# An encoder layer for two request groups: the sample's tiles first through attention and routing, its selection beside the prompt's out-projection

## What is computed

```python
h = rms_norm(x) ; p = h @ w_in
a = BiGLA(p[gla columns])            # 4 heads, chunked gated linear attention, both directions
d = DiffAttn(p[diff columns])        # 4 heads, softmax(q1 k1) - lam * softmax(q2 k2), rotary, QK-norm
x = x + concat(a, d) @ w_out
h2 = rms_norm(x)
aff = softmax(h2 @ w_router)         # 16 experts
gates, idx = top_k(aff.T, cap)       # per expert: 32 rows of the prompt, 64 of the sample
y[idx] += gates * (silu(h2[idx] @ w_gate) * (h2[idx] @ w_up)) @ w_down      # summed over 16 experts
```

## Time and profile before

| | us |
|---|---|
| median of 3 runs | 1534.68 (1534.57 to 1535.32) |
| the profiled execution | 1534.62 |
| its span | 1532.8 |
| PE busy | 1501.5 (98%) |
| DVE busy | 1245.4 (81%) |
| ACT busy | 1090.7 (71%) |
| POOL busy | 140.4 (9%) |
| mean of DMA traffic | 292 GB/s |

### The profile page before, as it was taken

One profiled execution on the slowest core, in us unless ns is written; L12 is line 12 of the kernel. 1 busy time (PEld: TensorE's weight loads), 2 busy tenths in 40 slices (PEclk: granted clock), 3 DMA queues, 4 the chain that ended last, 5 costly groups with the idle time before them and its releaser, 6 DMA issues.

```text
span 1532.8 us, 18601 instructions
## 1 busy us (share of the span) xinstructions
PE 1501.5 (98%) x7293; PEld 1228.2 (80%) x7293; DVE 1245.4 (81%) x1133; ACT 1090.7 (71%) x1230; POOL 140.4 (9%) x105
## 2 busy tenths in 40 slices
PE   7999999999999999999999999999999999999997
PEld 7787777678878888888888888888888888888886
DVE  4358679775588898888989888888988888898985
ACT  7555456875357878787787778778777878778784
POOL 1013131000000101010110101011010101101010
PEclk9999999999999999999999999999999999999999
DMA  6111101402759999999999999999999999999992
GB/s 233 56 55 56 56 1 56 154 28 81 269 200 389 376 388 372 396 374 393 380 384 384 378 395 377 393 380 385 383 378 394 380 393 375 390 383 385 393 375 74
DMA packets 191990, 447.98 MB, mean 292 GB/s; under 512 B 13016, under 2 KB 13344, under 8 KB 191904
## 3 DMA queue, kind: packets, MB, share of 16 engines
q1 hardware_dynamic: 187488, 433.03, 75.8%
q0 software_dynamic: 3968, 12.65, 3.6%
q10 hardware_dynamic: 448, 1.12, 0.2%
HBM read 434.19 MB, written 12.58 MB: 291 GB/s over the span
## 4 chain that ended last, share of the span: by engine, by line
PE 92%; DVE 4%; ACT 1%; issue 1%; DMA 0%; POOLq 0%; POOL 0%; DVEq 0%; ACTq 0%
PE ps L952 23%; PE ps L954 23%; PE ps L953 23%; PE ps L619 5%; PE ps L621 5%; PE ps L620 5%; PE ps L987 1%; PE ps L841 1%; PE ps L875 1%; DVE states L1502 1%; PE ps L945 1%; PE ps L861 1%; PE ps L897 1%; DVE slice_low L1410 1%; PE ps L927 0%
## 5 line engine op out<-in xcount | busy, mean ns | idle before, releaser
L1840 DVE TENSOR_TENSOR wl<-raw,wh 128x2048 fp32r<-128x2048 f32 x384 | 873.0, 2289 | 126.1 <-ACT wh L1345 124.6
L1345 ACT CAST wh<-raw 128x2048 fp32r<-128x2048 f32 x384 | 731.2, 1913 | 125.6 <-PE ps L954 123.5
L952 PE MATMUL ps<-wh,XTh 128*128 128x512 f32 x1024 | 404.9, 395 | 0.9 <-issue 0.9
L954 PE MATMUL ps<-wl,XTh 128*128 128x512 f32 x1024 | 399.5, 390 | 0.0
L953 PE MATMUL ps<-wh,XTl 128*128 128x512 f32 x1024 | 398.5, 389 | 0.0
L954 PEld LDWEIGHTS ps<-wl,XTh 128*128 128x128 f32 x1024 | 192.2, 188 | 41.1
L952 PEld LDWEIGHTS ps<-wh,XTh 128*128 128x128 f32 x1024 | 192.3, 188 | 38.8 <-issue 1.1
L953 PEld LDWEIGHTS ps<-wh,XTl 128*128 128x128 f32 x1024 | 192.5, 188 | 38.1
L952 PE MATMUL ps<-wh,gTh 128*128 128x512 f32 x512 | 200.9, 392 | 0.0
L954 PE MATMUL ps<-wl,gTh 128*128 128x512 f32 x512 | 199.5, 390 | 0.0
L953 PE MATMUL ps<-wh,gTl 128*128 128x512 f32 x512 | 199.2, 389 | 0.0
(11 more groups left out here) (244 smaller groups left out, 1573.0 us busy)
## 6 DMA issues: line engine op xcount, KB each, us to landing
raw<-in_w_gate SPq DMA_DIRECT2D x128, 1024.0 KB, 9.5
raw<-in_w_up SPq DMA_DIRECT2D x128, 1024.0 KB, 9.4
raw<-in_w_down SPq DMA_DIRECT2D x128, 1024.0 KB, 9.6
slice_raw<-in_w_in SPq DMA_DIRECT2D x5, 2048.0 KB, 8.0
X<-in_x_sample SPq DMA_DIRECT2D x8, 512.0 KB, 11.2
slice_raw<-in_w_out SPq DMA_DIRECT2D x2, 2048.0 KB, 8.8
X<-in_x_prompt SPq DMA_DIRECT2D x4, 512.0 KB, 4.4
slice_raw<-in_w_in SPq DMA_DIRECT2D x4, 512.0 KB, 7.8
```

What stands on the lines that cost most here:

```text
L952: pe.matmul(out, hi, rhs_h, start=first, stop=False)
L954: return pe.matmul(out, hi, rhs_l, start=False, stop=last)
L1345: act.copy(wh[:, n % CONV, :], raw[:, n % RAW, :]).then_inc(s_wh, 1)
L1840: dve.tensor_tensor(wl[:, n % CONV, :], raw[:, n % RAW, :], wh[:, n % CONV, :].bitcast(F32), ALU.subtract).then_inc(s_wl, 1)
```

## The change

The order of tiles becomes 2, 3, 4, 5, 0, 1 in the last projection slice, in the attention steps and in all that follows, and the tables are written anew for it. The sample's tiles have their out-projection (`dhalf`) inside the attention loop, and of the fills the prompt's first `turn` falls on iteration 22, its second on 26.

The prompt's four `half` pieces leave the loop. They stand behind it (`gla_half`), and the `dhalf` of the same tile adds on top of it in the same PSUM bank, so that one addition on DVE serves both. They alternate with the sample's `rows_turned` and logits. The softmax and the selection are made in two parts: the sample's eight rounds (64 partitions) stand on DVE between the additions, the root and the norm of the prompt's tiles; the prompt's four rounds (32 partitions) come last. The first round reads PSUM, without the copy that stood ahead of it. POOL lists the values that ACT listed. The rows are stored in two DRAM tensors, and each expert has two gathers, 64 rows and 32. `keep_busy` has 34 matmuls instead of 64. In the projections a third tile's turn comes one iteration later.

```diff
+ORDER = (2, 3, 4, 5, 0, 1)
-        21: ("half", 4, 1), 22: ("half", 5, 0), 23: ("half", 5, 1)}
-FILL[21].append(("dturn", 0, 0))
-FILL[23].append(("dturn", 1, 0))
-FILL.update({24: [("dhalf", 0, 0)], 25: [("dhalf", 0, 1)], 26: [("dhalf", 1, 0)], 27: [("dhalf", 1, 1)]})
...
+        18: [("dhalf", 2, 1)], 19: [("dturn", 4, 0), ("dhalf", 3, 0)], 20: [("dhalf", 3, 1)], 21: [("dhalf", 4, 0)],
+        22: [("dhalf", 4, 1), ("turn", 0, 0)], 23: [("dturn", 5, 0)], 24: [("dhalf", 5, 0)], 25: [("dhalf", 5, 1)],
+        26: [("turn", 1, 0)]}
...
-        return {3: (v0,), 4: (v0 + 1, v0 + 2)}.get(t, ())
+        return {3: (v0,), 4: (v0 + 1,), 5: (v0 + 2,)}.get(t, ())
...
-        ATT = [(g, h, t) for g in range(2) for t in range(GROUPS[g][1]) for h in range(HEADS)]
+        ATT = [(g, h, t) for g in (1, 0) for t in range(GROUPS[g][1]) for h in range(HEADS)]
...
+            pe.wait_ge(s_wtc, len(ATT))
+            gla_half(0, 0, LAST_BANK[0, 0], None)
+            rows_turned(3)
+            pe.wait_ge(*fill_read(last_in_bank(7)))
+            router_logits(2)
+            rows_turned(4)
+            router_logits(3)
+            rows_turned(5)
+            router_logits(4)
+            pe.wait_ge(s_pvc, len(ATT))
+            gla_half(0, 1, LAST_BANK[0, 1], None)
+            router_logits(5)
+            diff_turned(0)
+            pe.wait_ge(*fill_read(last_in_bank(6)))
+            gla_half(1, 0, LAST_BANK[1, 0], None)
             pe.wait_ge(s_aff, 1)
...
+            gla_half(1, 1, LAST_BANK[1, 1], None)
+            pe.wait_ge(s_mtd, POS[0] + 1)
+            diff_turned(1)
+            diff_half(0, 0, None)
+            diff_half(0, 1, None)
+            diff_half(1, 0, None)
+            rows_turned(0)
+            router_logits(0)
+            diff_half(1, 1, None)
+            rows_turned(1)
+            router_logits(1)
...
-            keep_busy(38)
...
-            keep_busy(26)
+            keep_busy(34)
...
+            affinity_exp(afft[:, :, 0:2, 0:NE], 1)
+            diff_high(1)
+            rows_squared(0)
+            h2_copied(0, 0)
+            h2_copied(0, 1)
+            rows_inverse_root(0)
+            rows_squared(1)
+            h2_copied(1, 0)
+            rows_inverse_root(1)
+            affinity_exp(afft[:, :, 2, 0:NE], 2)
...
+            for c in range(0, CAP_S, 8):
+                top_eight(both, c, ps[both, 7, 2 * P:4 * P] if c == 0 else aff[both, :], c // 8 + 1, c + 8 < CAP_S)
+                if c == 8:
+                    diff_low(1)
+                elif c == 16:
+                    diff_half_added(0, 0)
+                elif c == 24:
+                    diff_half_added(0, 1)
+                elif c == 32:
+                    root_refined(0)
                     rows_normed(0)
+                elif c == 40:
+                    diff_half_added(1, 0)
+                elif c == 48:
+                    diff_half_added(1, 1)
+            h2_copied(1)
...
+            for c in range(0, CAP_P, 8):
+                top_eight(rest, c, ps[rest, 2, 0:2 * P] if c == 0 else aff[rest, :], CAP_S // 8 + c // 8 + 1, c + 8 < CAP_P)
+            dve.transpose(pidx[0:CAP_P, :], topi[rest, 0:CAP_P]).then_inc(s_route, 1)
+            dve.transpose(gate[rest, :], topv[rest, 0:CAP_P]).then_inc(s_tables, 1)
```

More of the change, by code:

```diff
@@ L131, in link, with build @@
         self.own()
[L134 removed]
+def build(nc, a, y_prompt, y_sample, h2_prompt, h2_sample):
     ctx = ExitStack()
@@ L354, in build @@
                 b = 6 + u - (len(UNITS) - 2)
-            elif kind == "rope" and t % NT < 3:
+            elif kind == "rope" and t % NT < 2:
                 b = 6 + t % 2
             else:
-                b = sum(x[0] != "rope" or x[2] % NT >= 3 for x in UNITS[:u]) % 4
+                b = sum(x[0] != "rope" or x[2] % NT >= 2 for x in UNITS[:u]) % 4
             EARLIER.append(max((w for w in range(u) if BANKS[w] == b), default=None))
@@ L863, in _ @@
                     mm.then_inc(s_wt, 1)
+                if i == len(ATT) + 3:
+                    rows_turned(2)
                 if i >= len(ATT):
-                    for x in FILL[i]:
+                    for x in FILL.get(i, ()):
                         fill(x)
@@ L923, in _ @@
+            pe.wait_ge(s_aff, 2)
+            for j in range(2):
+                mm = pe.transpose(ps[0:GR, 2, j * P:(j + 1) * P], afft[:, j].rearrange("p g e -> p (g e)"), ident[:])
             mm.then_inc(s_afT, 1)
@@ new lines, in h2_copied, with affinity_exp @@
+            def h2_copied(v, f):
+                p = POS[v]
+                act.wait_ge(s_tr2, 2 * p + f + 1)
+                if p >= 2:
+                    act.wait_ge(s_lg, p - 1)
+                act.copy(h2T[p % 2][:, 4 * f:4 * f + 4, :], ps[:, 2 + f, :].rearrange("p (k c) -> p k c", k=4))\
+                    .then_inc(s_h2d if f else s_h2a, 1)
+            def affinity_exp(part, n):
+                act.wait_ge(s_lmx, n)
+                act.activation(part, part, ACT.Exp).then_inc(s_lex, 1)
@@ L1703, in beside @@
                         gla_half_added(x)
-                for x in FILL.get(i - 1, ()):
-                    if x[0] == "dturn":
+                    elif x[0] == "dturn":
                         diff_low(x[1])
@@ new lines, in _ @@
+            rows_normed(2)
+            h2_copied(4)
+            rows_normed(3)
+            h2_copied(5)
+            diff_mixed(1)
+            rows_normed(4)
+            rows_normed(5)
+            sample = afft[:, :, 0:2, 0:NE]
+            dve.wait_ge(s_clear, 2)
+            dve.wait_ge(s_lg, 4)
+            affinity_shifted(sample, logit[:, :, 0:2, 0:NE], root_of[:, :, 0:2].unsqueeze(3), stat_of[:, :, 0:2], 1)
+            diff_low(0)
+            affinity_scaled(sample, stat_of[:, :, 0:2], 1)
```

444 lines of the change are left out of this document (211 added, 233 removed).

## The result

| | before | after |
|---|---|---|
| median of 5 runs, us | 1535.32 (1534.57 to 1535.76) | 1540.25 (1538.44 to 1542.32) |
| ratio after / before | | 1.0035 [1.0024, 1.0046] |
| profiled execution, its span | 1534.62, 1532.8 | 1539.87, 1538.1 |
| last logits end | 417.80 | 434.06 |
| first expert matmul | 441.29 | 448.34 |

What follows compares the result with a forecast made beforehand. Expert stage on PE taken as fixed, so its first matmul's start decides: logits end 417.8 + (3.7 + 3.8 + 3.7 - 3.5) + 0.6 - 0.5 = 425.6, less 1.0, plus tail 15.7: 440.3 against 441.29. Forecast 1533.6 us, range 1528.8 to 1538.4.

Steps and rivals of the forecast that it cites:

- rival B: Clock falls to half at the attention's end and perhaps at the last logits: slower, 1536 to 1539.3 us; chance 0.20.
- Rival A: Overlap works: waits of iterations 22 to 24 and selection under half the sum, projections give 1 us; 1528 to 1531; chance 0.32.
- the attention's start: PE's waits for ACT's copies in sample steps 4, 5, 6 and 9: 3.7 us against 3.5 before, no gain.
- The projections: Third tile's turn an iteration later removes two PE waits for DVE, but ACT is late next: 0.5 us gained, 0 to 2.6.
- Iterations 22 to 24: End of the attention: three new PE waits on DVE and ACT (1.25, 1.15, 1.4), 3.8 us in sum.
- The selection: Sample's selection on DVE beside the prompt's out-projection: instruction order makes PE idle 0.3 + 0.3 + 1.75 + 1.35 = 3.7 us.
- The tail: From the last logits to the first expert matmul: 15.7 us after, 23.5 before, a gain of 7.8.
- Rounds: Prompt's four selection rounds in the tail: 1.50 us each on 32 partitions as on 96, the last 1.0; 5.5 us.
- the transposes: Two small transposes on DVE behind the prompt's rounds: 0.2 us taken, between 0.1 and 0.7.
- the prompt's gather: In the tail, 32 rows waited for instead of 96: 4.0 us taken, 3.5 to 4.5, against 4.54 before.
- the softmax and the merging: Tail's start: softmax of the prompt's logits with tile 1's norm, 3.0 us, and merging the sample's half lists, about 1.2.
- Rival C: Weight loads on SP delay the stores of `hn`, hence norms, sample's softmax and rounds: 1535.5 to 1538 us; chance 0.10.

Runs made afterwards that it cites:

- b1: The kernel before with 64 more thin matmuls (128x128 fp32 by 16 columns) among the turns and logits behind the attention; 1562.35 us against 1534.85 to 1534.99.
- e2: The changed kernel with the order of fills in iterations 17 and 19 swapped, `dhalf` first, then `dturn`; 1536.87 us, 1.0009 to before.
- g6: The changed kernel with the edits of e1, e2, e4 and s1 together; 1531.32 us, 0.9979 to before.
- e1: The changed kernel with `gla_half(0, 1)` ahead of the turn of tile 5 instead of behind the logits of tile 4; 1538.11 us, 1.0024 to before.
- e3: The changed kernel with the prompt's first `turn` in iteration 25 instead of 22; 1541.74 us, 1.0043 to before.
- g8: g6 with 12 matmuls, results overwritten, filling three of PE's waits in iterations 23 and 24; 1534.34 us, 0.9990 to before.
- k1: The changed kernel with 12 matmuls of 512 columns put between the logits of tile 3 and the turn of tile 5; 1539.42 us, 1.0030 to before.
- b2: The kernel before with 29 more matmuls of 128x128 by 512 columns, as control to b1; 1541.45 us, 1.0042 to before.
- e4: The changed kernel with tile 1's addition ahead of tile 0's root and norm on DVE, and the `h2T` copy ahead of the squares on ACT; 1538.02 us.
- s1: The changed kernel with SP's loads of weight tiles 0 to 2 behind the first two stores of rows; 1539.48 us, 1.0027 to before.

## Why the prediction was wrong

**The step that failed** is the last clause of "Work of PE between 262 and the logits' end is the same before and after; it moves. I therefore count only where PE does not do such work". The work was the same and took 6.6 us longer (4.8 and 1.8). The first of these lies at a place that no case had priced: I looked for the clock only beside idle time, since the fall in the routing of before stood behind a wait, and rival B priced the attention's end and the last logits (its sign, a clock below 1.00 between the attention's end and the logits, did come). Counting the idle time right was not enough; here the same work in another order ran at another speed. That thin work alone can do this is shown in the kernel before (b1); what set it off in the changed kernel, and why not in all of its variants, stays open. B was the nearest case, and too small: it had 3.4 us at most for the first fall, where 4.8 came. By its own terms its upper end is 1533.6 + 3.4 + 1.7 = 1538.7 and not 1539.3. Likewise A's 3.7 to 6 us give 1527.6 to 1529.9 and not 1528 to 1531, and the terms of the attention's start add up to 3.8, not 3.7; none of these changes the outcome.

**The second failure** is the 2.4 us in iterations 18 and 20. I had followed the pipeline hop by hop only from iteration 22, where the diff moves whole pieces, and had not asked at the others which bank each fill takes and who reads it. e2 shows it by its cure: both waits are gone from its trace.

**The projections**: 0.5 forecast, 0.05 came (attention starts at 262.14 against 262.19). Both waits for DVE's rotation went, but those for the next slice's low part rose from 1.4 to 3.1. The low end of my bounds, 0, was right.

**The attention's start**: 3.7 forecast, 2.7 measured. **Iterations 22 to 24**: 3.8 forecast (1.25 + 1.15 + 1.4), 3.6 measured (1.39 + 1.02 + 1.18); the trace names DVE and ACT for the first two, and for the third DVE's end 0.11 us earlier stands for it. **The selection**: 3.7 forecast, 3.0 measured (0.28 + 0.19 + 1.43 + 1.14), and DVE's wait for tile 0's root 2.70 where 2.8 was forecast. These are steps that held.

**The tail**: 15.7 forecast, 14.3 measured. Rounds are 1.5 us on 32 partitions as on 96, as I took; the transposes 0.20; the prompt's gather 3.35 (443.21 to 446.56) and not 4.0: less than the 3.5 that I had set as the least. The other 0.7 is the softmax and the merging: 3.5 us from the last logits to the first round (434.06 to 437.54), 4.2 forecast.

**Rival A** did not come, and its argument against itself held: each wait was an order of instructions. But the same orders could be changed, and then it is what g6 shows. **Rival C** was half there: DVE waited 2.8 and 1.1 us for stores of `hn` (named as a sign of C), but at a time when TensorE was late by its own fall. It came into view only where TensorE came earlier, in e1, e2 and e3 (2.5, 2.7 and 2.9).

**The Trainium skill**, page "TensorE: Matmul & The Clock Gate", section "HAM oscillation — how this bites in real kernels", ties the falls to waits between bursts. Here the clock fell in after's profile, in b1's and in g8's where PE had no idle time in the 16 us before; the measurement decides. By the rule I had given B less than the trace of before would have borne.

## What to carry to other kernels

When work is put in another order, look at what comes to stand next to each other on TensorE: turns and narrow matmuls in a row are a place where the clock can fall with no wait in sight. Wide matmuls between them went with shorter falls here, not with none, and e1 and k1, which put them in, gained less than the noise. Read the granted clock in windows over the whole stretch, and check it by the length of like matmuls, ahead of any explanation by waits. Compare the busy time of the same work, not only the idle time. Try each small wait's cure by itself and then all together: a wait that is hidden behind another loss shows no gain until that loss is gone.

## What the runs showed of the hardware

- Thin fp32 matmuls (16 columns) ran at the 1.2 GHz level for over 22 us on end with PE never idle (b1); 29 matmuls of 512 columns at the same place ran at 2.4 GHz (b2).
- In most of the changed kernels the runs with the higher mean clock are the faster ones: e4's two at 0.996 took 1533.7 and 1533.9, its eight others (0.991 to 0.994) 1536.9 to 1538.3. Most of these kernels spread over 3 to 7 us, the runs of before over 1.5 us.
- But the mean clock is no exact measure. g8's four runs at 0.994 took 1530.2, 1531.8, 1535.5 and 1535.5, and before's runs from 0.993 to 0.996 don't differ by it. One reason shows at the start: in before's profile and in after's, matmuls of 256 columns take 0.41 us until about 17 and 0.28 behind it, but the clock's row is 1.00 in the one and 0.60 in the other. Windows of before and of after, then before's timeline:

```profile
13.00:17.00 4.00, 3.58 (x17) 3.58 (x18) 3.89 (x8) 3.97 (x8) 0.00 (x0) 1.00 1.07 377
13.00:17.00 4.00, 3.58 (x18) 3.58 (x19) 3.96 (x8) 3.97 (x8) 0.00 (x0) 0.60 1.06 376
```

```profile
14.23 0.41 PE L619 MATMUL ps<-HTh,wih 128*128 128x256 f32 x1
17.59 0.28 PE L619 MATMUL ps<-HTh,wih 128*128 128x256 f32 x1
```

- An indirect gather of 32 rows of 4 KB took 3.35 us from the last index to PE's turn, one of 96 rows 4.54.
- MAX8, FIND_INDEX8 and MATCH_REPLACE8 (the three passes of a selection round) over 256 elements take 0.40 to 0.43 us each on 32, 64 and 96 partitions.
- Open: what decides in which runs the clock falls in a thin stretch; why e4's and s1's profiles had it fall at 377 to 381 and after's didn't, with the same waits in iterations 22 to 24.
